# In every attention unit TensorE takes the values of the unit two back ahead of the turns of the unit one back

## The reference, cut to what matters

```
s = q @ k^T            # scores, with a mask or a bias
p = exp(s - max(s))    # masked softmax
p = p / sum(p)         # (SWA: the sum has a sink term; NSA: times a gate)
o = p @ v              # values
```

## Time and profile before

| | |
|---|---|
| median of three runs | 2094.95 us (2093.49 to 2095.38) |
| profiled execution: time, span | 2093.4 us, 2091.7 us |
| PE busy | 2063.5 us, 99% of the span |
| DVE, ACT busy | 1079.3 us (52%), 823.0 us (39%) |
| chain that ended last | PE 82%, DVE 4%, ACT 1% |
| scores, turns, values (matmul groups) | L973, L990, L1011 |
| granted TensorE clock | 9 tenths or more in all 40 slices |

### The profile page before, as it was taken

How to read it: one execution, slowest core, us unless ns; L and a number is a source line. 1 busy time by engine, 2 the same in 40 slices (tenths; PEclk the granted TensorE clock), 3 DMA queues, 4 the chain that set the end, 5 groups by cost and what they waited for, 6 DMA issues and landing times.

```text
span 2091.7 us, 29775 instructions
## 1 busy us (share of the span) xinstructions
PE 2063.5 (99%) x11592; PEld 1737.7 (83%) x11592; DVE 1079.3 (52%) x1733; ACT 823.0 (39%) x1395; POOL 193.5 (9%) x168
## 2 busy tenths in 40 slices
PE   9999999999999999999999999999999999999998
PEld 7887788888888888889888888977888898888887
DVE  7557757343345646528443444837544545344344
ACT  7325644232233533325332232635554336223232
POOL 1001010200002002210300003502000211000000
PEclk9999999999999999999999999999999999999999
DMA  5222003233322322222332322322112222332321
GB/s 195 82 80 72 22 22 111 92 100 97 97 91 88 119 83 86 89 89 90 102 101 91 100 88 73 117 90 77 41 62 80 92 71 92 100 98 94 100 81 41
DMA packets 52052, 182.73 MB, mean 87 GB/s; under 512 B 5873, under 2 KB 8065, under 8 KB 51937
## 3 DMA queue, kind: packets, MB, share of 16 engines
q1 hardware_dynamic: 50112, 173.26, 26.0%
q0 software_dynamic: 1824, 7.85, 1.1%
HBM read 178.99 MB, written 2.10 MB: 87 GB/s over the span
## 4 chain that ended last, share of the span: by engine, by line
PE 82%; DVE 4%; ACT 1%; issue 0%; POOL 0%; ACTq 0%; DVEq 0%
PE ps L358 54%; PE ps L1028 5%; PE ps L1614 4%; PE ps L437 4%; PE ps L469 3%; PE ps L1692 3%; PE ps L973 2%; PE ps L1011 1%; PE ps L990 1%; PE ps L781 1%; DVE ring L331 1%; PE ps L1705 1%; PE ps L1659 1%; PE ps L1587 1%; DVE acc L555 1%; DVE h L560 1%
## 5 line engine op out<-in xcount | busy, mean ns | idle before, releaser
L358 PE MATMUL ps<-xa,ring 128*128 128x512 f32 x3240 | 748.7, 391 | 1.2 <-DVE ring L331 1.1
L358 PEld LDWEIGHTS ps<-xa,ring 128*128 128x128 f32 x3240 | 605.6, 188 | 130.5 <-issue 3.4
L324 ACT ACTIVATE ring<-raw 128x1024 fp32r<-128x1024 f32 x320 | 336.8, 1054 | 487.3 <-PE ps L358 392.2
L331 DVE TENSOR_TENSOR ring<-raw,ring 128x1024 fp32r<-128x1024 f32 x320 | 409.4, 1283 | 197.5 <-ACT ring L324 196.9
L358 PE MATMUL ps<-xb,ring 128*128 128x512 f32 x2208 | 502.6, 389 | 0.0
L358 PEld LDWEIGHTS ps<-xb,ring 128*128 128x128 f32 x2208 | 414.4, 188 | 86.1
L906 DVE TENSOR_TENSOR ffsq<-relu 128x512 f32<-128x512 f32 x96 | 66.4, 691 | 180.2 <-ACT relu L865 180.0
L923 DVE TENSOR_TENSOR acc<-acc,ps 128x512 f32<-128x512 f32 x68 | 46.8, 688 | 196.7 <-PE ps L358 196.7
L865 ACT ACTIVATE relu<-ps 128x512 f32<-128x512 f32 x64 | 38.1, 596 | 186.8 <-PE ps L358 185.6
L1028 PE MATMUL ps<-xa,ring 128*128 128x512 f32 x432 | 108.0, 400 | 0.0
L909 DVE TENSOR_TENSOR xb<-ffsq,xb 128x512 fp32r<-128x512 f32 x96 | 66.5, 692 | 75.8 <-ACT xb L857 75.8
(11 more groups left out here) (358 smaller groups left out, 2070.4 us busy)
## 6 DMA issues: line engine op xcount, KB each, us to landing
raw<-in_stream SPq DMA_DIRECT2D x320, 512.0 KB, 3.6
t<-in_rpb POOLq DMA_DIRECT2D x8, 448.0 KB, 6.0
h<-in_x SPq DMA_DIRECT2D x8, 256.0 KB, 5.9
c_w<-in_cmp_w POOLq DMA_DIRECT2D x4, 512.0 KB, 4.5
out_y<-h SPq DMA_DIRECT2D x16, 128.0 KB, 1.9
cons<-in_con SPq DMA_DIRECT2D x1, 610.0 KB, 8.2
raw<-in_stream SPq DMA_DIRECT2D x2, 256.0 KB, 3.7
wst<-in_w_s POOLq DMA_DIRECT2D x1, 512.0 KB, 3.7
```

What stands on the lines that cost most here:

```text
L324: nc.scalar.activation(ring[:, m % RING, 0], raw[:, m % RING], ACT.Copy).then_inc(hi_done, 1)
L331: nc.vector.tensor_tensor(ring[:, m % RING, 1], raw[:, m % RING], ring[:, m % RING, 0].bitcast(F32), ALU.subtract).then_inc(lo_done, 1)
L358: mm = nc.tensor.matmul(bank[:, :], ring[:, n % RING, w, k * P:(k + 1) * P], operand[:, k, xx], start=(start and i == 0 and w == 0 and xx ...
```

## The change

Two statements of `pe_attention` change places. In iteration i TensorE now issues scores of unit i, the work beside, the values of unit i-2, and then the turn of unit i-1. Nothing else is edited; all other engines have the same instructions in the same order.

```diff
@@ -1036,10 +1036,10 @@
                 if i < last:
                     pe_scores(pe, i)
                 beside(i - first)
+                if i - 2 >= first:
+                    pe_values(pe, i - 2, buffers[1])
                 if first <= i - 1 < last:
                     pe_turn(pe, i - 1, buffers[0])
-                if i - 2 >= first:
-                    pe_values(pe, i - 2, buffers[1])
 
         NMAX, SUM, SINK, DEN, REC, WGT, SINK_IN, MAX_IN = range(8)
```

## The result

The changed kernel takes 2106.14 us (median, 2105.37 to 2107.81) against 2094.92 us before in the same comparison: ratio 1.0057, 95% interval 1.0044 to 1.0069, slower. The forecast was 2107 us, 12.1 us above the kernel before; the medians lie 11.2 us apart.

What follows compares the result with a forecast made beforehand. TensorE's own stream was taken as the bound. NSA 2.2 + 2.5 - 0.5 + 1.3 = 5.5 us and NA with SWA 3.9 + 1.0 + 1.7 = 6.6 add 12.1 to 2094.95, giving 2107 us, range 2100 to 2113.

Steps and rivals of the forecast that it cites:

- Seams: Between TensorE's groups: a fourth change of form adds 0.14 us per paying iteration, 2.2 us in NSA, 3.9 elsewhere.
- The rival that this switch hides under the blocks: At TensorE's block matmuls: the array drains under their last columns, so switches cost nothing; time 2101; chance 12%.
- Hand-overs: At bank 2, first values of a pair wait for VectorE without the turn as filler: +2.5 us NSA, +1.0 NA.
- Drains: In the last two iterations of a row, copies of turns become exposed: +1.3 us in NSA, +1.7 in SWA.
- the rival of waiting copies: In 16 one-block NSA iterations, values wait for ScalarE's copies, half a microsecond each: +8 us, 2115; chance 9%.
- ends in narrow products that are a switch already: NSA iteration 12: its end already holds a change of form, so it was not counted as paying 0.14 us.
- TensorE's idle time should rise by some 6 us in NSA and 7: Sign in the profile after: TensorE idle some 6 us more in NSA, 7 in NA with SWA.
- the 16 and the 28: Iterations expected to pay 0.14 us each: 16 in NSA for 2.2 us, 28 in NA and SWA for 3.9.
- the first rival: At the turns: values ahead give VectorE time for norms, idle time of at most 10.4 us goes; 2090; chance 3%.
- the joined products: NSA iterations 27 to 29: L1536 and the values join in one form, one switch fewer each, -0.5 us.
- the second rival: At TensorE's block matmuls: changes of form cost nothing, only bank 2 waits and row ends stay; 2101; chance 12%.

Runs made afterwards that it cites:

- The last version: Kernel before, with values ahead in NSA iterations 27 to 29, VectorE's `out` first, GELU ahead of the copy, four blocks one iteration earlier; ratio 1.0003.
- the joined group: Kernel before, with one more unused group in the form of the values, between turn and values in 14 SWA iterations; ratio 1.0013.
- the early GELU: Changed kernel, with ScalarE executing the GELU of iteration 11 ahead of the copy of that iteration's turn; ratio 1.0064.
- the early `out`: Changed kernel, with VectorE reading bank 2 of a finished pair ahead of the maxima; ratio 1.0047 to the kernel before.

## Why the prediction was right

**Seams.** The step that carried half of the forecast was that an iteration goes from three changes of the array's form to four and that this costs 0.14 us. The profile after has 0.15 in 42 iterations, and three experiments hold it up: with little else left it makes the kernel slower (1.0035), with three changes of form the values can stand ahead of the turn for next to nothing, and one group costs 0.29 us more apart than joined. The rival that this switch hides under the blocks fell with these. It was findable beforehand only because iteration 28 happened to contain the new seams.

**Hand-overs.** Worked out at 0.76, 1.0, 0.7 and 1.0; measured 0.76, 1.03, 0.73 and 1.02. The sum held because a wait that was already there (unit 16, the NA pair) was not counted again: what is lost is the turn that used to fill it.

**Drains.** 1.3 and 1.7 against 1.22 and 1.61. TensorE's waits for L1071 are in the last two values of both rows and nowhere else, as said, so the rival of waiting copies did not occur in spite of its small margin.

**What missed.** "ends in narrow products that are a switch already" was right for the seam of iteration 12 and blind for its wait: ScalarE's copy of the turn comes later by the length of the values, and the GELU that TensorE waits for stands behind it in the queue, +0.43. I had looked for what waits for the copy and not for what is queued behind it. In iteration 25 the wait for the exponential takes up more than its own 0.14: it is 0.31 us shorter, as ScalarE and VectorE, which had been late in iterations 23 and 24, use their longer time (the maxima start 1.39 us behind the scores, 1.70 before). This gives back what those two had cost (0.15 and 0.16), and I have it from the timeline only. That the NSA row came out at 5.64 for 5.5 in spite of both is in part luck: +0.43 and -0.31 nearly cancel. And "TensorE's idle time should rise by some 6 us in NSA and 7" was wrong: it rose by 2.3 and 2.0, since seams are not idle time in this profile.

**Slips in the working.** Iteration 31 of each row is counted among the 16 and the 28 that pay a seam, though the drain, which starts from its blocks, has that seam already; without it the forecast is 11.8 us for 12.3 measured. Hand-overs and drains add up to 6.5 us and not 5.6, as the first rival has it, which puts that rival at 2091. And where seams cost nothing the joined products save nothing, so the second rival is at 2101.5. The 0.215 us for a block of values and the 0.16 fixed can't come from the one number that is given for them, 0.59; the trace before bears them out with 0.37 for one block and 1.02 for four.

## What to carry to other kernels

Before two groups on TensorE change places, count the changes of the array's form (rows by columns) around the loop in both orders, and price them from start to start, not by idle time; here one more cost 0.15 us, 42 times over. A piece of work behind a wait is its cover: at every hand-over and at the end of a pipeline, ask which group filled the wait, and count its full length. And on the engines whose input moves later, look at everything queued behind the moved instruction, not only at who waits for it.

## What the runs showed that was not expected

The granted clock of TensorE falls for a moment in some executions, behind a stretch in which TensorE pauses, and this costs more than most edits here. Around the start of NSA iteration 3 TensorE is busy for 2.0 of 4 us; the first fence shows this and the 5 us behind it in the kernel before, the second the same 5 us in the kernel with values before blocks, whose NSA row has the same instructions:

```profile
165.00:169.00 4.00, 2.01 (x24) 1.53 (x24) 3.18 (x9) 2.49 (x8) 3.12 (x4) 1.00 0.22 39
169.00:174.00 5.00, 5.00 (x52) 4.20 (x50) 4.86 (x11) 2.56 (x7) 0.00 (x0) 1.00 0.52 188
```

```profile
169.00:174.00 5.00, 5.00 (x41) 3.93 (x40) 4.80 (x10) 2.88 (x7) 0.00 (x0) 0.66 0.56 197
```

0.66 is a mean of stretches at the full 2.4 GHz and at half of it, 1.2 GHz. Iteration 3 took 6.61 us in place of 5.05, +1.56 for nothing that the kernel does. The last version shows the same (0.66, 6.59 us), and the joined group, the early GELU and the early `out` show it behind the wait of iteration 13 instead (0.66, 0.82 and 0.77 in 213:218, and in the latter two 0.84 and 0.89 in 218:223; iterations 13 and 14 together are longer than in a kernel of the same order by 1.54 to 1.57 in each). So a row's total from one execution can be off by 1.6 us by this alone, as much as the whole drain of SWA, and the iterations have to be compared one by one. The timed runs of the kernel before have such steps too: those with a mean granted clock of 0.999 took 2092.8 to 2094.1 us, those with 0.997 took 2096.4 to 2097.2. What decides in which execution it falls stays open.
